# First norm of a hybrid HGRN2 / RG-LRU step: the shift multiplied through the projection as two extra columns, scale's weights loaded first, 1/rms spread in two parts

## What is computed

```python
m = silu(cond) @ w_ada + b_ada                      # cond: c_ctx for context, c for latent tokens
sh1, sc1, g1, sh2, sc2, g2 = split(m, 6)            # 1024 columns each
h = rms_norm(x, norm1_gain) * (1.0 + sc1) + sh1
proj = h @ w_in                                     # 1024 x 4096
# two mixers read proj; then output projection, second norm, squared-ReLU MLP, final norm
```

## Time and profile before

| | us |
|---|---|
| median of three runs | 1792.59 |
| lowest, highest | 1792.48, 1793.4 |
| the profiled execution | 1793.19 |
| its span | 1791.3 |
| TensorE busy | 1680.2 (94%) |
| VectorE busy | 943.4 (53%) |
| ScalarE busy | 651.2 (36%) |

### The profile page before, as it was taken

How to read it: one execution, slowest core, us unless ns; L and a number is a source line. 1 busy time by engine, 2 the same in 40 slices (tenths; PEclk the granted TensorE clock), 3 DMA queues, 4 the chain that set the end, 5 groups by cost and what they waited for, 6 DMA issues and landing times.

```text
span 1791.3 us, 30956 instructions
## 1 busy us (share of the span) xinstructions
PE 1680.2 (94%) x13028; PEld 1403.8 (78%) x13028; DVE 943.4 (53%) x1355; ACT 651.2 (36%) x932; POOL 0.2 (0%) x4
## 2 busy tenths in 40 slices
PE   7799999989999996798999999999989999999997
PEld 5587887778778875687688888888878887877886
DVE  5702633643455257546876566665564444444436
ACT  3513327332823381345664544444440222022103
POOL 0000000000000000000000000000000000000000
PEclk8899999989999998899999999999999999999999
DMA  8544324332533244311322222223380222022102
GB/s 335 195 173 145 114 80 165 107 114 80 178 128 119 99 165 170 151 59 34 115 88 100 105 91 82 97 100 106 132 320 1 106 106 106 0 105 106 53 0 118
DMA packets 61550, 208.20 MB, mean 116 GB/s; under 512 B 8704, under 2 KB 17408, under 8 KB 59648
## 3 DMA queue, kind: packets, MB, share of 16 engines
q1 hardware_dynamic: 56400, 185.35, 28.5%
q10 hardware_dynamic: 5040, 21.22, 2.9%
HBM read 144.40 MB, written 62.13 MB: 115 GB/s over the span
## 4 chain that ended last, share of the span: by engine, by line
PE 47%; DVE 4%; ACT 1%; DMA 1%; issue 1%; DVEq 0%; SPq 0%
PE bank L95 15%; PE bank L97 15%; PE bank L96 15%; DVE hid_lo L1070 1%; DVE down_lo L1076 1%; DMA hid_raw<-hidden 1%; DVE x L1320 0%; PE bank L1250 0%; DMA hidden<-c 0%; DVE y_tok L1347 0%; DVE t_lo L1278 0%; PE bank L711 0%; ACT c L916 0%; DVE h_raw L1271 0%; DVE c L886 0%
## 5 line engine op out<-in xcount | busy, mean ns | idle before, releaser
L95 PE MATMUL bank<-h_hi,in_lo 128*128 128x512 f32 (+1 forms) x768 | 289.9, 378 | 12.4 <-issue 8.8
L95 PE MATMUL bank<-hid_hi,down_lo 128*128 128x512 f32 (+1 forms) x768 | 277.8, 362 | 20.8 <-DVE down_lo L1076 18.3
L96 PE MATMUL bank<-h_lo,in_hi 128*128 128x512 f32 (+1 forms) x768 | 277.1, 361 | 0.0
L97 PE MATMUL bank<-h_hi,in_hi 128*128 128x512 f32 (+1 forms) x768 | 276.6, 360 | 0.0
L1320 DVE SCALAR_TENSOR_TENSOR x<-bank,mod,x 128x512 f32<-128x512 f32 (+1 forms) x216 | 141.9, 661 | 254.5 <-PE bank L97 252.6
L97 PE MATMUL bank<-hid_hi,down_hi 128*128 128x512 f32 (+1 forms) x768 | 275.8, 359 | 0.0
L96 PE MATMUL bank<-hid_lo,down_hi 128*128 128x512 f32 (+1 forms) x768 | 275.3, 358 | 0.0
L95 PEld LDWEIGHTS bank<-hid_hi,down_lo 128*128 128x128 f32 x768 | 146.1, 190 | 45.6 <-issue 20.5
L95 PEld LDWEIGHTS bank<-h_hi,in_lo 128*128 128x128 f32 x768 | 148.7, 194 | 38.6 <-issue 14.9
L1677 ACT ACTIVATE mx_stage<-bank 128x512 f32<-128x512 f32 (+1 forms) x96 | 50.0, 524 | 348.9 <-PE bank L97 345.0
L96 PEld LDWEIGHTS bank<-h_lo,in_hi 128*128 128x128 f32 x768 | 149.1, 194 | 23.7 <-issue 5.0
(11 more groups left out here) (233 smaller groups left out, 2600.1 us busy)
## 6 DMA issues: line engine op xcount, KB each, us to landing
proj<-mx_stage ACTq DMA_DIRECT2D x32, 640.0 KB, 5.7
hid_raw<-hidden SPq DMA_DIRECT2D x32, 640.0 KB, 7.1
in_raw<-in_w_in SPq DMA_DIRECT2D x32, 512.0 KB, 6.1
mx_ada_raw<-in_w_ada_rest SPq DMA_DIRECT2D x32, 512.0 KB, 5.0
up_raw<-in_w_ff SPq DMA_DIRECT2D x32, 512.0 KB, 4.2
hidden<-c SPq DMA_DIRECT2D x64, 256.0 KB, 2.0
down_raw<-in_w_ff SPq DMA_DIRECT2D x32, 512.0 KB, 8.0
ada<-in_w_ada SPq DMA_DIRECT2D x8, 1024.0 KB, 20.0
```

Of the source, the lines that this page charges most:

```text
L95: nc.tensor.matmul(out, w_lo, x_hi, start=start, stop=False)
L96: nc.tensor.matmul(out, w_hi, x_lo, start=False, stop=False)
L97: return nc.tensor.matmul(out, w_hi, x_hi, start=False, stop=stop)
```

## The change

**Shift as two columns.** `h` no longer holds the shift. `h_hi` and `h_lo` get two columns more, ahead of the tokens, for the shift of context and latent tokens. `FirstNorm` makes x times 1/rms in VectorE in one operation a tile (`h_raw`, in the place of `h_lo`), ScalarE multiplies by amp and rounds, VectorE makes the rest. Each product with the context block takes 258 columns, so the first two columns of its bank are the shift times the weights; ScalarE copies them (`bias`) and adds them when it stages the tile's three blocks.

**Weights of scale first.** `w_ada` for scale (0.5 MB a tile) is loaded at the start and multiplied between the turns of chunks 6 to 9; that for shift is loaded behind the first weights and multiplied within the first products, after the fourth feature tile. The blocks with the context (258 columns) come last in the first products, and `modulation(0, 0)` comes behind them.

**1/rms in two parts.** The sums of chunks 0 to 5 are rooted, inverted and spread ahead of those of chunks 6 to 9.

**Other edits.** The spill of x moves from ahead of the slots to slot 2. The split of tile 2's weights stands at the beginning of slot 0 for both engines. Some buffers move by 128 bytes. The feed-forward is unchanged.

```diff
@@ start, SyncE
             for k in range(KT):
-                sp.dma_start(ada[:, k, :], a["w_ada"][k, :, :]).then_inc(ada_in[k], 16)
-            sp.wait_ge(turned, CHUNKS)
+                sp.dma_start(ada[:, k, :], a["w_ada"][1, k, :, :]).then_inc(ada_in[k], 16)
+            sp.wait_ge(turned, 7)
             for s in range(2):
                 sp.dma_start(g.in_ring.raw[:, s, :], a["w_in"][s, :, :]).then_inc(g.in_ring.raw_in[s], 16)
+            for k in range(KT):
+                sp.dma_start(g.shift_tiles[k][:, :], a["w_ada"][0, k, :, :]).then_inc(g.shift_in, 16)
@@ start, ScalarE, after the square of chunk c
+                if c == EARLY_CHUNKS + 1:
+                    take_root(0)
+                if c == CHUNKS - 2:
+                    act.wait_ge(conditioned, 1)
+                    act.wait_ge(zeroed, 1)
+                    for j in range(4):
+                        nc.scalar.activation(rows[32 * j:32 * j + 2, :], g.bank[4][32 * j:32 * j + 2, 0:REST], ACT.Copy
+                                             ).then_inc(rows_ready, 1)
+            for b in range(2):
+                spread_rows(b)
+            split_weights(nc, act, None, 0, 0, g.in_ring)
+            take_root(1)
+            split_weights(nc, act, None, 0, 1, g.in_ring)
+            spread_rows(2)
@@ start, TensorE
+            for c in range(CHUNKS):
+                turn(c)
+                if 2 <= c < EARLY_CHUNKS + 2:
+                    sums(c - 2)
+                if c >= EARLY_CHUNKS:
+                    for i in range(2):
+                        condition(2 * (c - EARLY_CHUNKS) + i)
+            sums(EARLY_CHUNKS)
+            sums(EARLY_CHUNKS + 1)
+            pe.wait_ge(rstd_ready, 1)
+            for b in range(2):
+                spread_block(b)
             pe.wait_ge(rows_ready, 4)
...
+            sums(CHUNKS - 2)
+            sums(CHUNKS - 1)
+            pe.wait_ge(rstd_ready, 2)
+            pe.wait_ge(moved, moves[CHUNKS])
+            spread_block(2)
@@ first norm, VectorE
+        def scale(k):
+            nc.vector.tensor_tensor(self.columns(g.h_raw, k, 0, TOKENS), g.x_first[:, k, :], g.rstd_all[:, :], ALU.mult
+                                    ).then_inc(self.normed, 1)
@@ first products, TensorE
+        for k in range(KT):
+            pe.wait_ge(self.lo_done, len(SEGS) * (k + 1))
             for s in range(2):
+                if k == 0:
+                    pe.wait_ge(w.lo_ready[s], 1)
+                for b in (1, 2):
+                    step(s, b, k)
+            if k == self.CONDITION_AFTER:
+                pe.wait_ge(g.shift_in, KT * 16)
+                for i in range(KT):
+                    last = condition_rows(nc, g, g.bank[self.ROW_BANK], g.shift_tiles[i], i, REST)
+                last.then_inc(self.conditioned, 1)
+            if k == self.TURN_AFTER:
+                pe.wait_ge(self.rows_ready, 4)
...
+        pe.wait_ge(self.shift_lo, 1)
         for s in range(2):
+            for k in range(KT):
+                step(s, 0, k)
@@ slots, SyncE
             def project(h, u, last):
+                if first(h) and u == 2:
+                    sp.dma_start(g.x_scratch, g.x_first[:, :, :].rearrange("p k t -> p (k t)")).then_inc(spilled, 16)
                 load_tiles(h, u)
...
-            sp.dma_start(g.x_scratch, g.x_first[:, :, :].rearrange("p k t -> p (k t)")).then_inc(spilled, 16)
@@ slots, ScalarE
-                nc.scalar.activation(stage[:, s, t0:t0 + n], g.bank[unit_bank(h, u)][:, 0:n], ACT.Copy
-                                     ).then_inc(staged[s], 1)
+                if b == 0:
+                    nc.scalar.activation(bias[:, s, :], g.bank[unit_bank(h, u)][:, 0:2], ACT.Copy).then_inc(bias_ready, 1)
+                    act.wait_ge(bias_ready, h * PER_HEAD + j + 1)
+                bank, c = g.bank[unit_bank(h, u)], int(b > 0)
+                nc.scalar.activation(stage[:, s, t0:t0 + n], bank[:, 0:n] if b else bank[:, 2:n + 2], ACT.Identity,
+                                     bias=bias[:, s, c:c + 1]).then_inc(staged[s], 1)
@@ slots, TensorE
+            norm.first_products(pe, FIRST_BANKS, lambda s, b: used[s] if b == 0 else unit_full[(0, 0, 1)[b]])
             modulation(0, 0)
-            norm.first_products(pe, FIRST_BANKS, lambda s, b: used[s] if b == 2 else unit_full[b])
```

More of the change, by code:

```diff
@@ L181, in _, with take_root, spread_rows @@
             nc.scalar.activation(cond_s[:, :, :], cond[:, :, :], ACT.Silu).then_inc(cond_ready, 1)
+            def take_root(part):
+                c0, c1 = PARTS[part]
+                act.wait_ge(summed, c1)
+                act.wait_ge(setup, 1)
+                nc.scalar.activation(root[:, c0:c1], g.bank[SUM_BANKS[part]][:, 0:c1 - c0], ACT.Sqrt, bias=g.eps[:, 0:1],
+                                     scale=1.0 / D_MODEL).then_inc(rooted, 1)
+            def spread_rows(b):
+                t0, n = TOK_BLOCKS[b]
+                act.wait_ge(spread, b + 1)
+                nc.scalar.activation(g.rstd_all[:, t0:t0 + n], spread_bank(b), ACT.Copy).then_inc(rstd_all_ready, 1)
             for c in range(CHUNKS):
@@ L304, in _ @@
                                            ).then_inc(mod_ready, 1)
+            invert(1)
             for s in range(2):
@@ L354, in scalar @@
     def scalar(self, act):
         nc, g = self.nc, self.g
-        with act.Fori(0, self.PAIRS) as i:
-            for s in range(2):
-                wait_apart(g, act, self.scaled[s], (i + 1) * len(SEGS))
-                for t0, n, c in SEGS:
-                    nc.scalar.activation(self.part(g.h_hi, i * 2 + s, t0, n), self.tmp[:, s, t0:t0 + n], ACT.Identity,
-                                         bias=self.shift(i * 2 + s, c)).then_inc(self.hi_done[s], 1)
-    def tensor(self, pe):
-        nc, g = self.nc, self.g
-        pe.wait_ge(self.rstd_ready, 1)
-        for b, (c0, kc) in enumerate(GROUPS):
-            for c in range(kc):
-                last = nc.tensor.matmul(g.bank[b][:, c * P:(c + 1) * P],
-                                        self.rstd[:, c0 + c:c0 + c + 1].broadcast_to([P, P]), g.ident[:, :],
-                                        start=True, stop=True)
-            last.then_inc(self.spread, 1)
@@ L394, in low @@
-        def low(i):
-            for s in range(2):
-                dve.wait_ge(self.hi_done[s], (i + 1) * len(SEGS))
-                for t0, n, c in SEGS:
-                    nc.vector.scalar_tensor_tensor(
-                        self.part(g.h_lo, i * 2 + s, t0, n), self.tmp[:, s, t0:t0 + n], self.shift(i * 2 + s, c),
-                        self.part(g.h_hi, i * 2 + s, t0, n).bitcast(F32), ALU.add, ALU.subtract
-                    ).then_inc(self.lo_done[s], 1)
-        scale(0)
-        with dve.Fori(1, self.PAIRS) as i:
-            low(i - 1)
-            scale(i)
@@ L408, in first_products @@
+        scale(0)
+        for k in range(1, KT):
+            scale(k)
+            low(k - 1)
+        low(KT - 1)
+        dve.wait_ge(self.rows_turned, 1)
+        modulation_add(nc, g, g.bank[self.ROW_BANK], REST, 0, 2).then_inc(self.shift_ready, 1)
+        dve.wait_ge(self.shift_hi, 1)
+        nc.vector.tensor_tensor(g.h_lo[:, :, self.SHIFT], g.mod[:, 0:8, :], g.h_hi[:, :, self.SHIFT].bitcast(F32),
+                                ALU.subtract).then_inc(self.shift_lo, 1)
     def first_products(self, pe, banks, signal):
@@ L426, in split_weights @@
+        pe.wait_ge(self.shift_lo, 1)
+        for s in range(2):
+            for k in range(KT):
+                step(s, 0, k)
 def split_weights(nc, act, dve, i, s, ring):
@@ L1682, in project @@
                                   ).then_inc(stored[s], 16)
-                if b == 0 and not (last and j == PER_HEAD - 1) and not (first(h) and j == 0):
+                if b == 0 and not (last and j == PER_HEAD - 1) and not (first(h) and j < 2):
                     split_weights(nc, act, None, h * (PER_HEAD // 2) + (j + 1) // 2, 1 - s, ring)
```

209 lines of the change are left out of this document (97 added, 112 removed).

## The result

| | before | after |
|---|---|---|
| median, us | 1792.53 | 1805.05 |
| lowest to highest (4 executions each) | 1792.27 to 1793.4 | 1804.14 to 1808.23 |
| ratio, 95% interval | | 1.0077 (1.006 to 1.0095) |
| span of the profiled execution | 1791.3 | 1802.3 |

The change makes the kernel 12.5 us slower. I forecast 1794.8, no measurable change; the time lies above my range.

What follows compares the result with a forecast made beforehand. TensorE, busy 94% of the span, was taken as the bound, with time to win ahead of its first product. Fourth tile 1.3 us later plus 0.9 for columns gave +2.2 on the median 1792.59: 1794.8, range 1787.5 to 1799.5.

Steps and rivals of the forecast that it cites:

- Part 1: Stretch ahead of the first norm: VectorE's first scaling starts near 40.1 against 51.83, 11.7 us earlier.
- the rival of a front that gives little: TensorE stays at half clock between the turns, everything behind is 4 us late: +6.2, 1798.8; chance 0.2.
- Part 2: First norm and first products: first low part ends near 44.7, TensorE bounds the 34.8 us behind it, modulation (0, 0) ends near 79.4.
- Part 3: Third tile, behind small constants and staging: starts at 81.5, 8.5 us earlier, and ends at 96.0.
- Part 4: Fourth tile's weights, queued behind the moved spill, land near 101.5; TensorE stands, the tile effectively starts at 105.8, 1.3 us later.
- Part 5: Two more columns in context products cost 0.9 us over 29 tiles; the bias costs nothing, at most 1 us.
- The rival that staging becomes late in the heads: Added copy and wait ahead of each context staging meet the mixing work: +3 to +7 us with the collision; chance 0.07.

Runs made afterwards that it cites:

- the last two runs: Changed kernel, spill ahead of the slots, context and latent rows in two tensors, run again: ratio 0.9969; the same with the second norm's rows too: 1782.23 us, 0.9936.
- the kernel with split rows and early spill: Changed kernel with context and latent rows in two tensors and the spill of x ahead of the slots: ratio 0.9979 to the kernel before, second run 0.9969.
- the kernel with split rows and late spill: Changed kernel with context and latent rows in two tensors, the spill of x left where the change has it: ratio 1.0036 to the kernel before.

## Why the prediction was wrong

**Part 1, the front: right.** First scaling 40.33, forecast 40.1. That it agrees to 0.2 is luck, as other traces of the same front lie between 37.8 and 41.2; the terms of the sum also make 37.0 and not the 37.3 that stands there. ScalarE copies the rows in 1.57 us from 32.07, the clock is 0.89 in 26 to 28 us, so the rival of a front that gives little did not come true.

**Part 2: right.** First product 44.87 for 44.7; modulation at 79.63 for 79.4 (the start of two tiles' worth, 1.05, so 0.8 late).

**Part 3: 1.6 late.** Third tile at 83.09 for 81.5. ScalarE starts behind the small constants at 78.33, not 77. From there it takes 4.8 us for the 4.5 forecast, as a staging with a bias is longer: three take 1.63, in the earlier trace rows 1.36.

**Part 4: right landing, wrong bound.** The weights landed at 101.5, the forecast number to the tenth (issued at 81.15, 20.3 us). That, too, is partly luck: the first transfer was issued at 80.30, not 79.4, and the 7.6 MB took 21.2 us, not 22.1. The step that failed is "The weights land near 101.5; high half ... make 103.9, 7.9 us after the third tile is done". The third tile was not done. I had put the stores into the bytes and not into the waits: they have a waiter too, ScalarE, which needs their half of `stage` back for the third tile. They land in 18 us since the queues take turns by packets, and the spill's are eight times as large. TensorE stands 6.5 us a block earlier, ahead of the third tile's last block, and that block comes behind the stand: 108.4 for 105.8, so +3.9 for +1.3. Of the 2.6 us between, 1.6 are those of part 3 and 1.2 the third tile's first block at the lower clock, which the 14.5 for that tile leave out; the stand and the clock behind it took less, 9.1 for 9.8, and the rest is small. The run with the weights first shows that they were not the bound, the one with the spill in pieces that the size of its packets made the stores late.

The Trainium skill ("DMA: Bandwidth & Descriptors", section "Queues, rings and completion order") says that each DMA engine goes round the queues it has work for and takes a whole packet from one before it turns to the next. The 17 packets each of 93 to 95 us agree. My prediction took from the same page a ceiling and that transfers of different engines interleave. The trace agrees with the interleaving, but that says nothing of shares.

**Part 5: the failed step is "The two-column rows of h cost nothing visible (the feed-forward's products have that layout already)".** I had put at nothing what costs up to 0.0049 us on each of 1392 products of 512 columns, 6.8 us. By the ratios it is 7.3 and 7.7 in the changed kernel and 4.1 in the kernel before; these agree within their intervals. The argument took the earlier trace rows, products of 258 columns, as proof for a layout whose cost lies in those of 512; the rows quoted above, 0.2311 on `h_hi` against 0.2274 on `t_hi`, were in the same trace. The 0.9 us for 258 columns is the right size or too much: with the pace restored a tile takes 14.49 us, before 14.51.

**The bias and the mixing: small, not settled.** The rival that staging becomes late in the heads was priced at 3 to 7 us. In the kernels with the change's arithmetic the lag grows by 3.8 to 4.2 us between the issues at 504 and 553 us (rows of before), by 1.9 and 2.5 in the last two runs; in those made from the kernel before it changes by -1.2 to +1.8. Timeline of TensorE at that place, in the kernel with split rows and early spill:

```profile
531.73 0.57 PE L1901 MATMUL bank<-mx_q,mx_k 128*32 128x32 f32 x41 [2.34 <-issue]
```

Before, no stand over 0.6 us is there between 520 and 550, but one of 3.1 at 513. The stand is ahead of a product of the mixing and is not put down to a staging; behind it the clock is at 0.57 in 532 to 536. From the fourth tile to the last, the lag of the four kernels with split rows grows by 0.1 to 2.9 us (from -7.9 to -6.7 in this one), that of kernels with the old arithmetic and the spacing of before changes by -0.4 to -2.1. Whether it is the copy and the wait ahead of each context staging, or only the new phase of the heads, no run tells.

**Sum.** Forecast +2.2: fourth tile +1.3, columns +0.9. In the trace of after: +3.9, and +7.5 up to the last modulation, of which the layout makes 5 to 7 (the kernel with split rows and late spill has 2.3 there). Without late spill and layout the change is worth 0.9979 to 0.9969, 3.8 to 5.6 us faster than before. The 8.5 us that the fourth tile could have started earlier, which I had seen eaten by the queue, were there to be had.

## What to carry to other kernels

Moving a long transfer means asking not only what is queued behind it on its own queue but who waits for each transfer on every other queue in that stretch, and how large the packets of each are. When a change moves tensors that TensorE reads, compare the spacing of the same products before and after over a whole tile: 2% in it is seen in no share of busy time. In a kernel like this one, keep moving rows and weight tiles at distances of a multiple of 256 bytes; where a row has to grow by a few columns, put the wide blocks in a tensor of their own.

## What the runs showed of the hardware

- The spacing of 512-column fp32r products follows the distance in SBUF between moving rows and weights: 0.227 us at shifts of 0, 256 or 512 bytes for all rows, 0.231 to 0.233 at 64 or 128 or when the distance changes by 8, 32 or 64 bytes from row to row. Moving both by 128 bytes changes nothing. The steady distance is 0.2266, and behind products of another distance or width it can take six to nine products to come back to it. I had expected nothing of addresses at all. That the unit is 256 bytes fits all runs; what in the chip makes it was not looked at.
- Two queues take turns packet by packet: 0.66 MB in 5 KB packets beside 5.24 MB in packets of 41 KB took 18 us, beside the same bytes in 5 KB rows 9.6. The price was issue time: six of the eight pieces took SyncE 7.64 us.
